# Interleaving output-projection slices with the next tile's first stage in the two mixer phases

## The reference, cut to what matters

```python
for i in range(DEPTH):                       # DEPTH = 2
    h = rms_norm(x, mix_norm_pre[i])
    m = conv_attn_mixer(h, ...) if i % 2 == 0 else short_conv_mixer(h, ...)
    x = x + rms_norm(m, mix_norm_post[i])    # m ends in "@ w_out", 1024 x 1024
    h = rms_norm(x, ffn_norm_pre[i])
    f = conv_glu_ffn(h, w_up[i], conv_w[i], w_down[i])
    x = x + rms_norm(f, ffn_norm_post[i])
```

## Time and profile before

| what | value |
|---|---|
| median of 3 runs | 5107.94 us (5071.97 to 5344.46) |
| the profiled execution, its own time | 4988.35 us |
| its span (slowest core, first to last instruction) | 4986.8 us |
| spans of the 8 cores | 4969.7 to 4986.8 us |
| busy share PE / DVE / ACT | 72% / 64% / 48% |
| ACT_TABLE_LOAD | 233 |

### The profile page before, as it was taken

One profiled execution on the slowest core, in us unless ns is written; L12 is line 12 of the kernel. 1 busy time (PEld: TensorE's weight loads), 2 busy tenths in 40 slices (PEclk: granted clock), 3 DMA queues, 4 the chain that ended last, 5 costly groups with the idle time before them and its releaser, 6 DMA issues.

```text
span 4986.8 us, 91242 instructions; the slowest of 8 cores (4969.7 to 4986.8 us)
## 1 busy us (share of the span) xinstructions
PE 3609.6 (72%) x31484; PEld 3027.2 (61%) x31484; DVE 3190.8 (64%) x7235; ACT 2383.2 (48%) x4688; POOL 53.8 (1%) x112
## 2 busy tenths in 40 slices
PE   3676767676744888888878477776717888888887
PEld 2555656564633777777767355665516776767676
DVE  4545455555534877778778456565528877778776
ACT  2334343434323766666667322222216766666665
POOL 1000000000000000000000000000010000000000
PEclk9787878787876888889889688888858989989888
DMA  5110101010128111211111433322281110110111
GB/s 103 27 54 27 54 27 54 27 54 27 44 46 153 27 49 29 52 34 44 52 26 45 81 74 77 77 58 70 61 146 39 52 52 27 52 51 28 52 35 39
DMA packets 228604, 264.61 MB, mean 53 GB/s; under 512 B 14256, under 2 KB 216240, under 8 KB 226096
## 3 DMA queue, kind: packets, MB, share of 16 engines
q1 hardware_dynamic: 214752, 207.88, 15.7%
q0 software_dynamic: 13392, 50.89, 6.1%
HBM read 241.46 MB, written 68.18 MB: 62 GB/s over the span
## 4 chain that ended last, share of the span: by engine, by line
PE 61%; DVE 16%; ACT 12%; issue 6%; DMA 2%; another core or an unknown queue 2%; DVEq 1%; ACTq 0%; POOL 0%; SPq 0%; POOLq 0%
PE ps L293 45%; PE ps L292 16%; ACT sq L303 5%; DVE tmp L318 4%; DVE stat L326 3%; DVE yy L318 3%; DVE xr L307 3%; ACT L303 2%; DVE tmp L307 1%; DMA WA<-w3in 1%; DMA xp<-xsA 1%; DVE WA L312 1%; ACT stat L303 1%; ACT ya L303 1%
## 5 line engine op out<-in xcount | busy, mean ns | idle before, releaser
L293 PE MATMUL ps<-h,WAF 128*128 128x256 bf16 (+2 forms) x11968 | 1451.7, 279 | 214.8 <-DVE tmp L318 169.5
L293 PEld LDWEIGHTS ps<-h,WAF 128*128 128x128 bf16 x11968 | 1174.3, 102 | 408.3 <-issue 230.7
L326 DVE RECIPROCAL stat<-stat 128x256 f32<-128x256 f32 (+3 forms) x204 | 348.3, 1707 | 859.1 <-ACT stat L303 859.0
L318 DVE SCALAR_TENSOR_TENSOR yy<-ub,smallt,yy 128x254 f32<-128x254 f32 (+2 forms) x1496 | 702.5, 470 | 159.8 <-DVE yy L318 5.0
L303 ACT ACTIVATE ya<-ps,smallt 128x254 f32<-128x254 f32 (+2 forms) x1496 | 693.7, 464 | 171.0 <-ACT ub L303 2.6
L293 PE MATMUL ps<-sq,ones 128*128 128x256 bf16 (+2 forms) x1156 | 208.5, 341 | 780.9 <-ACT sq L303 725.2
L292 PE MATMUL ps<-actc,WAF 128*128 128x254 bf16 (+2 forms) x5984 | 730.6, 269 | 19.2 <-DVE tmp L318 17.3
L318 DVE SCALAR_TENSOR_TENSOR yy<-ub,smallt,ya 128x254 f32<-128x254 f32 (+2 forms) x1496 | 693.9, 464 | 52.3 <-PE ps L293 32.9
L293 PE MATMUL ps<-h,WA 128*128 128x256 bf16 (+1 forms) x5984 | 664.5, 272 | 52.6 <-DVE tmp L318 27.7
L293 PEld LDWEIGHTS ps<-h,WA 128*128 128x128 bf16 x5984 | 574.5, 99 | 134.3 <-issue 64.8
L293 PEld LDWEIGHTS ps<-sq,ones 128*128 128x128 bf16 x1156 | 124.6, 118 | 845.6 <-issue 813.5
(11 more groups left out here) (84 smaller groups left out, 2363.6 us busy)
## 6 DMA issues: line engine op xcount, KB each, us to landing
xp<-xsA SPq DMA_DIRECT2D x32, 1024.0 KB, 8.7
xr<-xsA SPq DMA_DIRECT2D x32, 1024.0 KB, 6.0
WAF<-wup POOLq DMA_DIRECT2D x16, 1408.0 KB, 45.6
xp<-xT SPq DMA_DIRECT2D x17, 1024.0 KB, 8.8
xr<-xT SPq DMA_DIRECT2D x17, 1024.0 KB, 7.5
xsA<-xr SPq DMA_DIRECT2D x17, 1024.0 KB, 6.6
xp<-xsB SPq DMA_DIRECT2D x16, 1024.0 KB, 11.6
xr<-xsB SPq DMA_DIRECT2D x16, 1024.0 KB, 6.2
```

The source lines that it names most:

```text
L293: return S.add("pe", lambda e, o=out, l=lhsT, r=rhs, a=start, b=stop: e.matmul(o, lhsT=l, rhs=r, start=a, stop=b), reads, writes)
L318: e.scalar_tensor_tensor(out=o, in0=a, scalar=s, in1=b, op0=p0, op1=p1), reads, writes)
L326: return S.add("dve", lambda e, o=out, i=in_: e.reciprocal(out=o, in_=i), reads, writes)
```

## The change

A new driver, run_pipeline3, takes the place of run_pipeline in the two mixer phases. B is split into its 8 slices (8 matmuls each, one K chunk into all 4 banks) and a final part (norm_residual and the store). A1 calls tick() after each of its pieces: phase 1 after V, after each of 6 rotary projections, and after each of 8 score blocks; phase 3 twice in each of its four chunks. Each tick emits one slice; the tick of the 8th slice also emits the final part. The load of xr stands ahead of A1(i+1). prep(i+2) moves from between A1(i+1) and B(i) to behind the final part of tile i.

```diff
+        def run_pipeline3(nt, prep, A1, A2, bslices, bfinal):
...
+            st = {0: prep(0)}
+            A1(0, st[0], noop)
+            if nt > 1:
+                st[1] = prep(1)
+            A2(0, st[0], noop)
+            for i in range(nt):
+                pending = bslices(i, st[i])
+                state = {'idx': 0, 'done': False}
+
+                def tick(i=i, pending=pending, state=state):
+                    if state['done']:
+                        return
+                    pending[state['idx']]()
+                    state['idx'] += 1
+                    if state['idx'] == len(pending):
+                        bfinal(i, st[i])
+                        state['done'] = True
+
+                if i + 1 < nt:
+                    A1(i + 1, st[i + 1], tick)
+                while not state['done']:
+                    tick()
+                del st[i]
+                if i + 2 < nt:
+                    st[i + 2] = prep(i + 2)
+                if i + 1 < nt:
+                    A2(i + 1, st[i + 1], noop)
...
             pfree(bk)
+            tick()
...
                 rope(2048 + g * 128, 2304 + g * 128, krot[g][:, 128:128 + n], b_krot[g])
+                tick()
...
                 qr_t.append((qt, qb))
+                tick()
...
                         pTs[(g, b, half)] = (p_t, p_b)
+                        tick()
...
-            out_proj_norm_residual(kch, lambda k, m: WA1[:, W1OUT + k * D + m * 128: W1OUT + k * D + (m + 1) * 128],
-                                   xt, xb, n, 0, SC_GAIN + (1 * 2 + 0) * 8, s)
+            banks, sl = out_proj_slices(kch, lambda k, m: WA1[:, W1OUT + k * D + m * 128: W1OUT + k * D + (m + 1) * 128], n, 0)
...
+        def p1_bfinal(ti, st):
+            s, n = st['s'], st['n']
+            xt, xb = st['xr']
+            norm_residual(st['banks'], xt, xb, n, 0, SC_GAIN + (1 * 2 + 0) * 8, s)
             store_x(xt, xb, xsA_v, "xsA", s, n, s)
 
-        run_pipeline(ntiles1, prep1, p1_A1, p1_A2, p1_B)
+        run_pipeline3(ntiles1, prep1, p1_A1, p1_A2, p1_bslices, p1_bfinal)
...
                     TT("dve", cu[:, 0:n], psum[bk][:, 256:256 + n], usb[:, 0:n], ALU.mult, [pbufs[bk], usbb], [cub])
                     pfree(bk)
+                    tick()
...
                     st['ybs'].append((yb_, ybb))
-
-            def p3_B(i, st):
+                    tick()
...
-            run_pipeline(len(tiles), prep3, lambda i, st: chunks3(st, 0, 4), lambda i, st: chunks3(st, 4, 8), p3_B)
+            run_pipeline3(len(tiles), prep3, lambda i, st, tick: chunks3(st, 0, 4, tick), lambda i, st, tick: chunks3(st, 4, 8, tick),
+                          p3_bslices, p3_bfinal)
```

More of the change, by code:

```diff
@@ L474, in run_pipeline2, with noop @@
                 del st[i]
+        def run_pipeline3(nt, prep, A1, A2, bslices, bfinal):
+            if nt == 0:
+                return
+            def noop():
+                pass
+            st = {0: prep(0)}
[8 more added lines that the diff above has]
+                    if state['done']:
+                        return
+                    pending[state['idx']]()
[12 more added lines that the diff above has]
+                    A2(i + 1, st[i + 1], noop)
         ph1 = es.enter_context(ExitStack())
@@ L550, in prep1, with p1_A1 @@
             return dict(s=s, n=n, h=h, hb=hb, Cf=Cf, Cfb=Cfb, Sf=Sf, Sfb=Sfb)
-        def p1_A1(ti, st):
+        def p1_A1(ti, st, tick):
             s, n, h, hb = st['s'], st['n'], st['h'], st['hb']
@@ L610, in p1_A1, with p1_A2 @@
                         pTs[(g, b, half)] = (p_t, p_b)
+                        tick()
             st['pTs'] = pTs
             st['proj_into'] = proj_into
-        def p1_A2(ti, st):
+        def p1_A2(ti, st, tick):
             s, n, h, hb = st['s'], st['n'], st['h'], st['hb']
@@ L711, in p1_A2, with p1_bslices @@
             st['mixk'] = achunks + ochunks
-        def p1_B(ti, st):
+        def p1_bslices(ti, st):
             s, n = st['s'], st['n']
-            xt, xb = load_x(xT_v, None, s, n, xr_rot)
+            st['xr'] = load_x(xT_v, None, s, n, xr_rot)
             mixk = st['mixk']
             kch = [(mixk[k][0][:, 0:n], mixk[k][1], wout_b[k]) for k in range(8)]
-            out_proj_norm_residual(kch, lambda k, m: WA1[:, W1OUT + k * D + m * 128: W1OUT + k * D + (m + 1) * 128],
-                                   xt, xb, n, 0, SC_GAIN + (1 * 2 + 0) * 8, s)
+            banks, sl = out_proj_slices(kch, lambda k, m: WA1[:, W1OUT + k * D + m * 128: W1OUT + k * D + (m + 1) * 128], n, 0)
+            st['banks'] = banks
+            return sl
+        def p1_bfinal(ti, st):
+            s, n = st['s'], st['n']
+            xt, xb = st['xr']
+            norm_residual(st['banks'], xt, xb, n, 0, SC_GAIN + (1 * 2 + 0) * 8, s)
             store_x(xt, xb, xsA_v, "xsA", s, n, s)
-        run_pipeline(ntiles1, prep1, p1_A1, p1_A2, p1_B)
+        run_pipeline3(ntiles1, prep1, p1_A1, p1_A2, p1_bslices, p1_bfinal)
         ph1.close()
@@ L842, in prep3, with chunks3 @@
                 return dict(s=s, n=n, h=h, hb=hb, ybs=[])
-            def chunks3(st, c0, c1):
+            def chunks3(st, c0, c1, tick):
                 n, h, hb = st['n'], st['h'], st['hb']
@@ L873, in chunks3, with p3_bslices, p3_bfinal @@
                     st['ybs'].append((yb_, ybb))
-            def p3_B(i, st):
+                    tick()
+            def p3_bslices(i, st):
                 s, n, ybs = st['s'], st['n'], st['ybs']
-                xt, xb = load_x(xsB_v, "xsB", s, n, xr_rot)
+                st['xr'] = load_x(xsB_v, "xsB", s, n, xr_rot)
                 kch = [(ybs[k][0][:, 2:n], ybs[k][1], w3out_b[k]) for k in range(8)]
-                out_proj_norm_residual(kch, lambda k, m: WA3[:, W3OUT + k * D + m * 128: W3OUT + k * D + (m + 1) * 128],
-                                       xt, xb, n, 2, SC_GAIN + (1 * 2 + 1) * 8, s)
+                banks, sl = out_proj_slices(kch, lambda k, m: WA3[:, W3OUT + k * D + m * 128: W3OUT + k * D + (m + 1) * 128], n, 2)
+                st['banks'] = banks
+                return sl
+            def p3_bfinal(i, st):
+                s, n = st['s'], st['n']
+                xt, xb = st['xr']
+                norm_residual(st['banks'], xt, xb, n, 2, SC_GAIN + (1 * 2 + 1) * 8, s)
                 store_x(xt, xb, xsA_v, "xsA", s, n, s + 2)
-            run_pipeline(len(tiles), prep3, lambda i, st: chunks3(st, 0, 4), lambda i, st: chunks3(st, 4, 8), p3_B)
+            run_pipeline3(len(tiles), prep3, lambda i, st, tick: chunks3(st, 0, 4, tick), lambda i, st, tick: chunks3(st, 4, 8, tick),
+                          p3_bslices, p3_bfinal)
             ph3.close()
```

## The result

The change makes the kernel slower: 5516.98 us median (5415.54 to 5688.77, 9 runs) against 5096.15 us (5047.97 to 5344.46, 10 runs), a ratio of 1.0687 with a 95% interval of 1.0617 to 1.0757. The profiled execution took 5417.18 us, on its own level 1.086 times that of before: 429 us more. The runs of before began at 5047.97 us where its profile took 4988.35, those of after at 5415.54 where its profile took 5417.18, which is why the two ratios differ; what set the runs of before apart from their profile was not tried. Timed again beside the experiments, the shortest run of before took 4984 to 4991 us in three rounds and 5016 in the fourth.

What follows compares the result with a forecast made beforehand. The prediction took waits between engines, none of them full, to bound the kernel; +249 us in phase 1 and +204 in phase 3 made +453, 5441 us on the profiled execution, 5560 on the runs' level, range 5380 to 5650.

Steps and rivals of the forecast that it cites:

- SP's queue as the view that decides: Both mixer phases: SP works in code order, so the xp load behind a tile's store cannot leave before the residual ends.
- (a): Phase 1, xp load's issue to prep's norm matmuls, with positions' landing and angle work no longer hidden: 17.3 us.
- (b): Phase 1, prep's norm matmuls to the convolution's start, through h and abuf on DVE: 10.9 us.
- (c): Phase 1, convolution's start to the first mix tile: 34.0 us.
- (d): Phase 1, from the first mix tile: rotary and slice matmuls after PE's stop at slice 0, cold clock, score block: 20.0 us.
- (e): Phase 1, the last slice behind score block 0, whose Exp stands on ACT ahead of the four Squares: 3.9 us.
- (f): Phase 1, residual's norm matmuls to the next xp load's issue, including a table load for Sqrt: 12.9 us.
- X to A2: Phase 3, xp load's issue to A2's first matmul: landing 11.6, Square 1.9 and 0.1, cold norm matmuls 1.7; 15.3 us.
- the cheap rival: Cheaper waits: phase 1's angle wait 11.0 us instead of 17.3, phase 3's load landing in 8.8; 5425 us, chance 22%.
- the signs named ahead: PE waits for xp's Square of over 20 us in each phase 3 tile, 15 or more in phase 1, among others.
- The dear rival (banks): Both mixer phases: four banks held through A1, or PE's lower clock, cost 3 us more a tile; 5650 us, chance 10%.
- The faster rival: Mixer phases: slice matmuls fill PE's stops and nothing new waits, 6.9 us a tile gained; 4887 us, chance 3%.

Runs made afterwards that it cites:

- the kernel with the loads early: Changed kernel with prep(i+2)'s loads (xp, in phase 1 also positions) issued at the head of iteration i, ahead of store(i); ratio 1.025 to the kernel before.

## Why the prediction was right

The direction and the mechanism were right; of the sizes, two errors cancelled in part. The sum was +453 us on the profiled execution, 429 came. The median was forecast at 5560 us and came at 5516.98: 24 us of the difference are the sum's, the other 20 the level of the runs, which lay 99.8 us above the profile and not 120. Nothing in the prediction derived that level; that it came so near was luck.

- SP's queue as the view that decides: shown, by two kernels that take the load out from behind the store in different ways and agree to 0.2 us.
- Phase 1's tile, 99.0 forecast, 99.5 measured. Its steps, read in the tile shown above: (a) 16.4 for 17.3, as the positions left 0.56 us behind xp and not 0.96 and landed in 7.8 instead of 8.4; (b) 10.8 for 10.9; (c) 33.3 for 34.0, the convolution ran at the higher clock throughout (granted clock 1.00) and took 13.75 us (the prediction's 13.4 was a slip: 124 matmuls at 10.64 us for 96 are 13.7); (d) 20.9 for 20.0; (e) 3.9 for 3.9; (f) 14.2 for 12.9. In (f) I had taken the residual's norm matmuls at their old 1.03 us. In this tile they follow a stop of 3.75 us and took 1.87, which is 0.8 of the 1.3 missing.
- The first store came 10.0 us earlier (11 forecast). What the sum lacked is the last tile: 70.2 us against 60.1. There no prep follows, but the gated projection, which ran under the residual before, comes behind it and behind the score blocks. That is 10 of the missing 21 us; another 10 are the tile, which grew by 18.0 and not 17.3 us, over 15 tiles. So phase 1 was +270 and not +249.
- Phase 3's tile, 60.1 forecast, 57.2 measured over 14 tiles, 57.9 in the one shown. The step that was mis-sized is X to A2: 13.0 us for 15.3, as the load landed in 9.1 us instead of 11.6. The other steps: 30.5 for 30.7, 2.4 for 2.5, 11.9 for 11.6. The short tile cost 6 us and not 15: with the full tile's terms I had not counted that a small load lands sooner (5.3 us) and its Square is short (0.44 us). The first store came 12 earlier. So phase 3 was +154 and not +204; the bound of 8.8 us for the landing, put under the cheap rival, was nearer than the median that I took. The other half of that rival did not come: in phase 1 the angle still waited for the positions, and (a) was 16.4 us, not 11.0.
- Of the signs named ahead, the stops of over 20 us in phase 3 came in each full tile (20.5 to 22.9). Those of 15 or more in phase 1 did not: four of the first tiles had them (15.1 to 17.8), most had 12.9 to 13.5. The score blocks, held up by banks, ran on until 3.4 us behind the issue of xp in the tile shown, so less of (a) was left for PE to stand.
- The feed-forward phases: 0 forecast, +5 measured, unexplained and small.
- Table loads: 263, as forecast. The ones in the row of steps cost 1.28 us each; in the changed kernel too the next operation follows at once (load 772.13, Exp 773.42), so the drain that the Trainium skill adds to a switch (ScalarE: Activation LUTs, What ACT_TABLE_LOAD costs) does not show here.
- The dear rival (banks): the four held banks do stop PE, 0.7 us at each of several score blocks and 5.4 once in a tile of phase 1, but beside the residual, where nothing waits for PE. In phase 3 they cost 1.8 us in the tile shown and less in others, inside the 30.7.
- The faster rival: its first half is true in phase 3. Slices that fill PE's stop bring 3.1 us a tile, if prep stays where it was. Interleaving by itself was worth having in one phase of two.

## What to carry to other kernels

When a step is moved in a program whose queues run in the order of the code, follow its DMA first: whatever stands ahead of it in the issuing queue is now ahead of it in time, and a store waits for the end of the work. A load belongs where its buffer comes free, not where its data are used. And before splitting work into slices look at which input is ready last: the slice that comes first should be the one whose input is oldest (here that alone gave back 2.6 us of the 99.5).

## What the runs showed of the hardware that was not expected

- A store to DRAM issued from POOL's queue cost this kernel no more than one from SP's: 0.89 us on the queue against 0.36, 5.1 us to landing in phase 1 and 8.8 in phase 3 (from SP, in the kernel before, 6.6 and 7.3), and the tiles were those of the kernel with the loads early, to 0.2 us.
- The same 1 MB load landed sooner in the changed kernel: xp<-xsB 9.1 us against 11.6, xp<-xT 8.0 against 8.8. It follows the store by 0.5 us in both, and no run here tells why.
- PE's clock fell in a shorter stop than I had reckoned with, but not in every one of its kind. After the stops of 3.69 to 3.86 us in phase 1 the residual's eight norm matmuls took 1.86 or 1.87 us in seven of 15 tiles, 1.03 in four and something between in four; after those of 2.30 to 2.69 us in phase 3 they took 1.03 in 11 of 15 and 1.57 to 1.85 in four. So the length of the stop alone did not decide it. One of the tiles that kept the clock:

```profile
1268.41 1.03 PE L293 MATMUL ps<-sq,ones 128*128 128x256 bf16 x8 [3.69 <-ACT sq L303]
```

- In a window from 751.90 to 757.10, behind the stop at slice 0, the granted clock was 0.50, the 1.2 GHz level; the 16 matmuls of a rotary projection took 3.62 us there and 1.91 later. The Trainium skill (TensorE: Matmul & The Clock Gate, Why this matters for your kernels) warns of idle gaps between bursts of matmuls for this reason. The trace agrees with it in the main: the clock fell in 11 of the 15 longer stops and in 4 of the 15 shorter ones.
